# Two filler matmuls before the last three turns of the probabilities, and the convolution's steps one earlier, in a two-layer hybrid decoder step

## What is computed

```
hn = rmsnorm(xp, norm_mix[l])
q_nope, q_rope, c_kv, k_r, qb, kb, vb, g = project_in(hn, ...)
a_out = mla_prompt(q_nope, q_rope, c_kv, k_r, w_ukv[l])         # 6 heads, causal
b_out = combine_dilations([dilated_prompt(qb, kb, vb, w, d) ...])# 6 heads, 3 dilations
c_out = conv_module(g_ext, conv_w[l], conv_b[l], conv_ln_g[l], conv_ln_b[l])
xp = xp + concatenate([a_out, b_out, c_out]) @ w_out[l]
xp = xp + peer_blocked(rmsnorm(xp, norm_ffn[l]), ...)            # 128 x 128 experts
```

```
y = lax.conv_general_dilated(g_ext, conv_w[:, None, :], (1,), 'VALID', ...) + conv_b
return jax.nn.silu(layernorm(y, ln_g, ln_b))
```

## Time and profile before

| | us |
|---|---|
| median of 3 runs | 2097.25 |
| lowest, highest | 2097.09, 2101.16 |
| the profiled execution, device time | 2097.09 |
| its span | 2095.3 |
| PE busy | 2070.9 (99%) |
| DVE busy, ACT busy | 1573.4 (75%), 1280.7 (61%) |

### The profile page before, as it was taken

The page is one execution under the profiler, slowest core; times in us unless marked ns, Lnnn a source line. Parts: engine busy times, 40 slices in busy tenths (PEclk is TensorE's granted clock), DMA queues, the critical chain, the costliest instruction groups (busy, mean ns, idle before and its releaser), DMA issues.

```text
span 2095.3 us, 40740 instructions
## 1 busy us (share of the span) xinstructions
PE 2070.9 (99%) x15552; PEld 1798.3 (86%) x15552; DVE 1573.4 (75%) x3566; ACT 1280.7 (61%) x2521; POOL 125.4 (6%) x138
## 2 busy tenths in 40 slices
PE   9999999999999999999999999999999999999998
PEld 7766799999999888788886658999999998887886
DVE  6874589867899776666677746898688997766766
ACT  5355445658888655565563544456688876655654
POOL 2200010000000010100022000100000001101000
PEclk9999999999999999999999999999999999999999
DMA  9453437776666898898664434477766668988876
GB/s 323 151 157 122 144 134 255 247 254 222 214 219 209 287 307 292 301 323 276 232 224 162 146 137 146 161 258 248 251 211 215 220 214 297 316 288 290 265 261 217
DMA packets 141841, 481.77 MB, mean 230 GB/s; under 512 B 26034, under 2 KB 48594, under 8 KB 135232
## 3 DMA queue, kind: packets, MB, share of 16 engines
q1 hardware_dynamic: 129248, 438.45, 62.3%
q0 software_dynamic: 10496, 40.42, 5.6%
q10 hardware_dynamic: 1904, 0.29, 0.1%
HBM read 475.82 MB, written 104.21 MB: 277 GB/s over the span
## 4 chain that ended last, share of the span: by engine, by line
PE 97%; DVE 2%; ACT 0%; issue 0%; DMA 0%; DVEq 0%; ACTq 0%
PE ps L1170 35%; PE ps L1217 33%; PE ps L863 4%; PE ps L823 3%; PE ps L907 3%; PE ps L1182 3%; PE ps L1133 2%; PE ps L915 2%; PE ps L1141 1%; PE ps L1137 1%; PE ps L872 1%; PE ps L1001 1%; PE ps L1156 1%; PE ps L1004 1%; PE ps L1017 1%; PE ps L967 1%
## 5 line engine op out<-in xcount | busy, mean ns | idle before, releaser
L2140 DVE TENSOR_TENSOR parts<-region,parts 128x1024 fp32r<-128x1024 f32 x512 | 625.8, 1223 | 301.7 <-ACT parts L1463 299.7
L1170 PE MATMUL ps<-tokens_hi,parts 128*128 128x256 f32 x4096 | 760.5, 284 | 0.0
L1463 ACT CAST parts<-region 128x1024 fp32r<-128x1024 f32 x512 | 538.6, 1052 | 271.0 <-PE ps L1217 214.5
L1217 PE MATMUL ps<-parts,parts_hw 128*128 128x512 f32 x3072 | 699.6, 389 | 0.0
L1217 PEld LDWEIGHTS ps<-parts,parts_hw 128*128 128x128 f32 x3072 | 575.7, 188 | 126.0 <-DVE parts_hw L2190 6.9
L1170 PEld LDWEIGHTS ps<-tokens_hi,parts 128*128 128x128 f32 x4096 | 636.7, 188 | 1.0 <-issue 0.5
L1170 PE MATMUL ps<-parts_hw,parts 128*128 128x256 f32 x2048 | 573.7, 280 | 0.0
L1170 PEld LDWEIGHTS ps<-parts_hw,parts 128*128 128x128 f32 x2048 | 386.5, 189 | 0.0
L1509 ACT ACTIVATE big<-ps 128x256 f32<-128x256 f32 (+31 forms) x252 | 131.7, 522 | 147.0 <-PE ps L1170 146.9
L1497 ACT CAST parts_hw<-big 128x256 fp32r<-128x256 f32 x256 | 171.0, 668 | 0.7 <-DVE big L2201 0.7
L1490 ACT ACTIVATE region<-region 128x128 f16<-128x128 f16 x512 | 169.2, 436 | 0.0
(11 more groups left out here) (324 smaller groups left out, 2225.3 us busy)
## 6 DMA issues: line engine op xcount, KB each, us to landing
region<-in_peer_uT SPq DMA_DIRECT2D x256, 512.0 KB, 4.1
region<-in_peer_v SPq DMA_DIRECT2D x256, 512.0 KB, 4.7
out<-in_state_win_k SPq DMA_DIRECT2D x112, 384.0 KB, 4.8
out<-in_state_win_v SPq DMA_DIRECT2D x112, 384.0 KB, 5.0
big<-in_state_win_k SPq DMA_DIRECT2D x48, 192.0 KB, 2.7
big<-in_state_win_v SPq DMA_DIRECT2D x48, 192.0 KB, 4.1
region<-in_w_out SPq DMA_DIRECT2D x4, 2048.0 KB, 8.1
big<-in_peer_wq SPq DMA_DIRECT2D x4, 2048.0 KB, 13.8
```

Of the source, the lines that this page charges most:

```text
L1170: mm = pe.matmul(ps[:, j % ZB, 0:SEQ], a, hp[b][:, c, :], start=(c == 0 and n == 0), stop=(c == KD - 1 and n == 2))
L1217: mm = pe.matmul(ps[:, 2 * half + t, :], w_t[a][:, 128 * t:128 * t + 128], v_t[b][:, 512 * half:512 * half + 512], start=(j == 0 and n == ...
L1463: act.copy(hi_t[n % HIGHS], rows_t[n % ROWS]).then_inc(high[l], 1)
L2140: dve.tensor_tensor(lo_t[n % ROWS], rows_t[n % ROWS], hi_t[n % HIGHS], ALU.subtract).then_inc(low[l], 1)
```

## The change

`turn_probs` gets two filler matmuls before its wait for the exponentials, for the heads 9, 10 and 11, that is in the steps 10, 11 and 12 of each layer. All five entries of `CONV_STEP` are one lower.

```
-CONV_STEP = (8, 9, 10, 11, 12)
+CONV_STEP = (7, 8, 9, 10, 11)
@@
                 def turn_probs(u):
+                    if u >= 9:
+                        keep_busy(("PT", u), 2)
                     pe.wait_ge(exp_ready, u + 1)
                     turn("PT", u, parts=[(prob[:, u % 2, 128 * i:128 * i + 128], 128, 128, 128 * i) for i in range(3)])
```

## The result

The changed kernel took 2115.58 us in the median of 4 runs (2110.43 to 2119.59); the kernel before, with the runs beside it, 2097.81 us. The ratio is 1.0081 with a 95% interval of 1.0055 to 1.0105. That is 17.8 us slower. The forecast was slower, 2110.1 us with a range of 2104.5 to 2114.5: the sign is right and the size is too small, the median lies 1.1 us above the range.

The account below looks back on a forecast made before the run. PE was taken to bound the kernel (97% of the chain). Per layer +5.46 fillers, +1.9 PP, -0.85 wait of step 10 give +6.5 us; two layers, +13.0 on 2097.09, give 2110.1 us, range 2104.5 to 2114.5.

Parts of the forecast that it names:

- Fillers: Steps 10 to 12: each pair adds 1.82 us on PE, 5.46 us per layer, 10.9 us in all.
- The sign named for it: In the profile after, L853 would show 40 instead of 28 instructions.
- `yt` and the wait of step 10: Moving yt from step 9 to 8 removes PE's wait at head 10's scores: -0.85 us per layer.
- `samples_conv`: Step 8: moved ahead of DVE's read of head 8's scores, it makes PP wait, +1.9 us per layer.
- Statistics, root, normalisation: One step earlier, with a second table load on ACT; PE does not wait in steps 11 and 12: cost zero.
- The clock: End of the mixing stage: the 5.1 us lost to low clock stay as they are.
- rival 2: Step 8: the clock falls anew around PE's two waits, 1.7 us per layer, 2111.8 or 2113.5 us; chance 0.20.
- Rival 1: End of the mixing stage: fillers keep the clock up, giving back 5.1 us, 2105.0 us; chance 0.17.
- Rival 3: Ahead of the three turns: fillers run in PE's idle time, 10.9 us given back, 2096 to 2098 us; chance 0.05.
- Rival 4: Step 8: PP does not wait, since DVE is ahead; 3.8 us less, 2106.3 us; chance 0.08.

Follow-up runs that it names:

- experiment 1: The kernel before plus only the six pairs of filler matmuls, CONV_STEP as before: 2112.03 us, +10.9, ratio 1.0053 to the kernel before.
- experiment 2: The changed kernel without its filler lines, so only the five CONV_STEP entries one lower: 2109.66 us, +8.5, ratio 1.0037 to the kernel before.
- experiment 11: The kernel before with only samples_conv one step earlier and filler matmuls in both PE waits of step 8: 2101.44 us, +3.4, ratio 1.0015.
- experiment 3: The kernel before with only samples_conv one step earlier, no fillers: 2115.49 us, +14.3, ratio 1.0072.
- experiment 5: The changed kernel run again, nothing altered: 2124.53 us in 6 runs, ratio 1.0089 to the kernel before.
- experiment 8: The kernel before plus two fillers, one in its old step 8 wait and one ahead of olT: 2104.46 us, +0.8, ratio 0.9999.
- experiment 10: The kernel before with one filler in its 1.0 us wait of step 8, nothing else: 2097.97 us, ratio 1.0000.

## Why the prediction was right and where it was wrong

- **Fillers, +10.9: right.** Alone they measured +10.9 (experiment 1), each pair 1.82 us in the trace, none hidden. The sign named for it was miscounted: L853 has 28 instructions before and 52 after, since six pairs are 24 (four each), not 12.
- **`yt` and the wait of step 10, -0.85 per layer: right.** The wait is gone in the changed kernel, and without fillers a wait of 0.6 us for the exponentials takes its place (experiment 2; 0.5 predicted).
- **`samples_conv`, +1.9 per layer: right,** a wait of 1.76 in every layer that has it and a delay of `PP` of 1.93. With PE kept busy in it, this edit costs 3.4 us in all (experiment 11).
- **Statistics, root, normalisation, zero: right** in the trace: the table load is there, no wait of PE follows.
- **The clock, counted at no change: wrong,** and this is the step that failed. The sum left the low stretches as they were and put a fall in step 8 at nothing. I saw the mechanism, as rival 2, and its place, but gave it 0.20 and 1.7 us per layer. I leaned on one row at 231 us with a full clock (called an idle second there; it is one microsecond, PE busy for 1.02 of 2.00 us), for a place with two waits of together 2.8 to 3.3 us within about 4 us. And I priced a fall by the shortest low stretch of the one trace, 3.4 us, where the runs have up to 10.2 us. Measured: 5.7 us in experiment 2 (8.5 - 2.8), about 5 in the changed kernel (17.8 - 13.0), 10.7 in experiment 3 (14.3 - 3.6). That the profiled execution came out at the forecast was luck: it lacked 6.8 us of low clock that the one of before had elsewhere. The Trainium skill ("TensorE: Matmul & The Clock Gate", HAM oscillation) has idle gaps throttle the clock again, but it speaks of gaps longer than any here; that two shorter ones in a row are enough is what experiments 3 and 11 show.
- **Rival 1, the clock holds at the end: wrong.** The fillers in steps 10 to 12 and the one ahead of `olT` leave the low stretches behind them where they were (experiments 1, 5 and 8).
- **Rival 3** is out: the fillers run in no idle time but the 0.6 us per layer of step 10, which the sum had counted. **Rival 4** is out: `PP` waits.

What stays open: why experiment 3 lost more to the clock than experiment 2 (20.3 against 13.5 us in the mean), with the same wait in step 8. It keeps the wait of 0.85 us in step 10, and its profile has 10.2 us of low clock at the stage's end, but nothing was run on that. Whether the new wait alone is enough or needs the old one ahead of it was not run either: no kernel has the new wait unfilled with the old one filled. Open too is which execution gets how many falls: one program had 17 and 44 us of them.

No version beat the kernel before. The free filler (experiment 10) equals it.

## What to carry to other kernels

Work that is moved ahead of a result which PE is about to need becomes a PE wait, and such a wait can be priced twice: by its length, and by the matmuls that run at half speed behind it. Here the 1.76 us wait close behind one of 1.0 to 1.5 us was priced so, and the shorter one alone was not. Where a wait can't be avoided, matmuls into a free bank inside the wait cost nothing and took the second price away here (10.9 us of 14.3). The same matmuls where PE does not wait cost their full length and bought nothing.

## What was not expected of the hardware

One program's runs scatter mostly by the granted clock: the changed kernel from 2118.28 to 2130.49 us on one chip, and the kernel before from 2097.62 to 2116.29 on it, but 2094.27 to 2101.06 on another. Up to the last matmul a low stretch lasted 3.4, 6.8 or 10.2 us, and nothing between, in all 13 profiles. And the clock also fell with no idle time ahead: behind the short matmuls at the end of the mixing stage, as at 194.8 us in the earlier trace rows, in 12 of 13 profiles, though not in that of experiment 11, whose clock stayed full to the end of both stages. What decides there was not tested.
